# The first Strassen product of each MLP, computed ahead of the plain second matmul

## The chip, the core and the metric

The kernel runs on one core of a Trainium2 chip. The metric is device time in microseconds (us), the median of the timed runs; before the change it is 1533.13 us. Engines are named as in the profile: PE is TensorE, DVE VectorE, ACT ScalarE, POOL GpSimd, SP the queue that issues nearly all DMAs. Each engine works off its own instructions strictly in order and waits on semaphores.

## The reference

Two trunk layers run over 512 latent and 128 context tokens (640 in all, width 1024, float32). Layer 0 mixes tokens by convolution and retention, layer 1 by attention; each then has a squared-ReLU MLP, and only that is touched here:

```python
m = jax.nn.silu(cond) @ ada_w[layer] + ada_b[layer]      # six vectors of 1024: shifts, scales, gates
sh1, sc1, g1, sh2, sc2, g2 = ...
h = rmsnorm(x, norm_g[layer, 1]) * (1 + sc2) + sh2
x = x + g2 * (jnp.square(jax.nn.relu(h @ mlp_w1[layer])) @ mlp_w2[layer])   # 1024 -> 4096 -> 1024
```

The product `silu(cond) @ ada_w` of layer 1, and the gates of layer 0, are computed in small pieces between the other matmuls of layer 0. Layer 1 has none left to compute.

## The kernel before

**Three products for one.** A float32 number is kept as a high part (`wH`, `hH`, `fH`; type fp32r) and the rest (`wL`, `hL`, `fL`). A product is high·high + high·low + low·high, three matmuls. ACT copies the high part, DVE or POOL subtracts it from the raw number to get the low part. A group of 12 such matmuls of 320 columns (4 row blocks x 3) fills one PSUM bank.

**The MLP in cycles.** The 4096 hidden columns are taken in eight cycles of 512 (`CYCLES`). Cycle 0 is plain: `w1(0)`, eight groups that make 512 hidden columns, then `w2(0)`, sixteen groups that multiply them back. Cycles 1 to 6 compute both products by Strassen's scheme, with seven block products each: those on the first matrix are keyed `("p", s, i)`, those on the second `("q", s, i)`, where `i` is B11, T2, T3, T1, B22, B21, T4 in PE's order for p. T1 to T4 are sums of weight blocks that DVE makes (`add_blocks`, L2588). A p product is 24 matmuls. The last cycle is p products and a plain second matmul. The very first p product of a layer is B11 times A11 (upper left block of h); it depends on h alone, and not on the hidden columns.

**From `w1(0)` to `w2(0)`.** ACT takes the ReLU of a group (`relu`, L1770), DVE squares it (`fs`, L2522), ACT copies the high part (`hidden_hi`, L1764), DVE subtracts (`hidden_lo`, L2513, writes `fL`). The loop `hidden` on DVE does this for eight pieces n = 0 to 7; at n = 5 it also makes the low parts of tile t0+2 (the first of the two tiles of `w2(0)`; `weight_lo`, L2221), at n = 6 the first sum of h blocks (`s_raw`, L2533). PE takes piece n = 7 in the third group of `w2(0)`. After that DVE adds each of the sixteen groups to x (`update`, L2087) and between them makes the sums and low parts that the p products need (the table `after`).

**Before the fifth p product.** B22 shares banks 0 and 1 with T1, so PE may start it only when DVE has read T1's result (`combine`, L2604, writes `fq`). On DVE's list that comes behind `t_lo` of T1, B22 and B21, the sum for T4, and the first sum for the next group (`q_add(s2, T3)`, writes `t_first`), which waits for a weight block loaded into the buffer that p's B22 has freed.

**Buffers.** Raw weights land in four buffers (`raw` holds 0 and 1, `raw_high` 2 and 3), dealt in turn; high and low parts have four slots each, dealt in turn by `BLOCK_AT`. `load_raw` makes SP wait until the low part of the buffer's previous block is there.

**The ada pieces.** `ada` is one buffer of 1 MB. `load_ada(p)` (L567) waits until piece p-1 has been used; `strips(p)` on PE (L875, 16 matmuls) waits for its landing. In layer 0 pieces 16 and 17 are used behind groups 5 and 7 of `w1(0)` (`hooks`), piece 18 in the middle of `w2(0)`, and then some in every cycle. In SP's code `ada_block(1)`, which is piece 17, stands behind all four loads of `w2(0)`.

Of the kernel before, what the change touches and what calls it, by code (L numbers as in the profile page):

```python
# [46 lines left out]
PLAIN = 1  # L47
# [26 lines left out]
T_MLP0 = T_WC + 2  # L74
# [12 lines left out]
Q_ORDER = (B11, T2, T3, T4, T1, B22, B21)  # L87
SUM_ORDER = (T3, T2, T1, T4)
P_DVE = ((T1, B22, B21, T4), (T2, T3, T1, B22, B21, T4))
BLOCKS, RAW_SEQ = [], []  # L90


# [5 lines left out]
for t_ in range(N_TILES):  # L98
    layer_ = 0 if T_MLP0 <= t_ < T_QKV else 1
    c_, b_ = divmod(t_ - (T_MLP0, T_MLP1)[layer_], 4)  # L100
    if not (T_MLP0 <= t_ < T_QKV or T_MLP1 <= t_) or b_ < 2 and c_ < PLAIN or b_ > 1 and c_ not in W2:
        BLOCKS += both(t_)
        RAW_SEQ += both(t_)
    elif b_ == 0:
        BLOCKS += [("p", WINO * layer_ + c_ - PLAIN, i_) for i_ in range(7)]
        RAW_SEQ += [("p", WINO * layer_ + c_ - PLAIN, i_) for i_ in (B11, T1, B22, B21)]
    elif b_ == 2:
        BLOCKS += [("q", len(W2) * layer_ + c_ - PLAIN, i_) for i_ in Q_ORDER]
        RAW_SEQ += [("q", len(W2) * layer_ + c_ - PLAIN, i_) for i_ in (B11, T1, B22, B21)]
# [2 lines left out]
RAW_BUF, RAW_COUNT, RAW_PREV, raw_last_, raw_n_ = {}, {}, {}, [None] * 4, 0  # L112
for key_ in RAW_SEQ:
    if key_[0] in ("p", "q") or T_MLP0 <= key_[0] < T_QKV or T_MLP1 <= key_[0]:
        buf_ = raw_n_ % 4
        raw_n_ += 1
    else:
        buf_, raw_n_ = 2 * (key_[0] % 2 and key_[0] in TWO_RAW) + key_[1], 0
    RAW_BUF[key_], RAW_PREV[key_] = buf_, raw_last_[buf_]
    RAW_COUNT[key_] = 1 + (RAW_COUNT[raw_last_[buf_]] if raw_last_[buf_] else 0)  # L120
    raw_last_[buf_] = key_
# [140 lines left out]
def hybrid_step(nc, x_prompt, x_sample, state_ret, cache_k, cache_v, ada_w, even_w_in, even_w_out, final_g,  # L262
# [3 lines left out]
    with ctx:  # L266
# [274 lines left out]
        def _(sp):  # L541
# [83 lines left out]
            def load_mlp(layer, first_tile):  # L625

                def w1(c):
                    for b in range(2):
                        load_tile(first_tile + 4 * c + b, k8(mlp_w1[layer], 512 * c + 256 * b))
                        if layer == 0 and c == 0 and b == 0:  # L630
                            load_ada(M_MLP)

                def w2(c, tile, js):
                    if c < CYCLES - 1:
                        halves = [mlp_w2[layer, 512 * c:512 * (c + 1), 256 * q:256 * (q + 1)]
                                  .rearrange("(k p) n -> p k n", p=P) for q in (2 * tile, 2 * tile + 1)]
                    else:
                        halves = [mlp_w2[layer, 512 * c + 256 * (1 - j):512 * c + 256 * (2 - j), 512 * tile:512 * (tile + 1)]
                                  .rearrange("(k p) n -> p k n", p=P) for j in range(2)]
                    load_tile(first_tile + 4 * c + 2 + tile, halves, js)  # L640

                def p_block(c, row, col):

                    return (mlp_w1[layer, 512 * row:512 * (row + 1), 512 * c + 256 * col:512 * c + 256 * (col + 1)]
                            .rearrange("(k p) n -> p k n", p=P))

                def q_block(c, row, col):

                    return (mlp_w2[layer, 512 * c + 256 * row:512 * c + 256 * (row + 1), 512 * col:512 * (col + 1)]
                            .rearrange("(k p) n -> p k n", p=P))  # L650

                def ada_block(n):

                    if layer == 0:
                        load_ada(M_MLP + n)

                def first_blocks(c):

                    s = WINO * layer + c - PLAIN
                    load_raw(("p", s, B11), p_block(c, 0, 0))  # L660
                    load_raw(("p", s, T1), p_block(c, 0, 1))
                    load_raw(("p", s, B22), p_block(c, 1, 1))
                    ada_block(3 * c)
                    load_raw(("p", s, B21), p_block(c, 1, 0))

                def second_blocks(c):

                    s = len(W2) * layer + c - PLAIN
                    load_raw(("q", s, B11), q_block(c, 1, 0))
                    load_raw(("q", s, T1), q_block(c, 1, 1))  # L670
                    ada_block(3 * c + 1)
                    load_raw(("q", s, B22), q_block(c, 0, 1))
                    load_raw(("q", s, B21), q_block(c, 0, 0))
                    ada_block(3 * c + 2)

                w1(0)
                for c in range(CYCLES):
                    if c in W2:
                        second_blocks(c)
                    else:  # L680
                        if 0 < c < PLAIN:
                            ada_block(3 * c)
                        w2(c, 0, (0,))
                        if c == CYCLES - 1:
                            ada_block(3 * c + 1)
                        w2(c, 0, (1,))
                        w2(c, 1, (0,))
                        if 0 < c < PLAIN:
                            ada_block(3 * c + 1)
                        w2(c, 1, (1,))  # L690
                        if c == 0:
                            ada_block(1)
                        ada_block(3 * c + 2)
                    if c + 1 < PLAIN:
                        w1(c + 1)
                    elif c < CYCLES - 1:
                        first_blocks(c + 1)
# [49 lines left out]
        def _(pe):  # L747
# [436 lines left out]
            def first_strassen(layer, c, v, part):  # L1184
# [3 lines left out]
                def one(i, operand, bank, m, opens=True):  # L1188
                    block_product(("p", s, i), 256, 4, bank, m, operand, opens)

                wait_low(pe, "p", s, B11)
                for m in range(2):
                    if c - 1 in W2:
                        pe.wait_ge(dve_free, v - 28 + 22 + m)
                    one(B11, A11, 6 + m, m)
                part(0)
                wait_low(pe, "p", s, T2)
                pe.wait_ge(s_ready, 4 * layer + 1)
# [75 lines left out]
            def mlp(layer, norm):  # L1274
# [6 lines left out]
                for c in range(CYCLES):  # L1281
                    t, v, s = t0 + 4 * c, v0 + V_CYCLE[c], WINO * layer + c - PLAIN
                    hooks = {}
                    if c == 0:
                        if layer == 0:
                            hooks = {5: [lambda: strips(M_MLP)], 7: [lambda: strips(M_MLP + 1)]}
                        tile_pair(t, hH, hL, lambda n: pe.wait_ge(dve_free, v0 - 3 + n) if n < 4 else pe.wait_ge(act_free, a0 + n - 3),
                                  lambda half, tile, k: pe.wait_ge(h_ready, 16 * norm + 8 * half + k + 1), hooks,
                                  inside=(2, 0, lambda: stat(norm, 1, SUMS)), joint=((0, 1), (2, 3), (4, 5), (6, 7)))
                    elif c < PLAIN:  # L1290
                        for b in range(2):
                            if layer == 0:
                                hooks = {1: [lambda c=c, b=b: strips(M_MLP + 3 * c + b)]}
                            tile_t(t + b, hH, hL, lambda n: pe.wait_ge(dve_free, v - 3 + n) if b == 0 else
                                   pe.wait_ge(act_free, a0 + 8 * c + n + 1), None, hooks)
                    else:
                        first_strassen(layer, c, v, part(c))
# [166 lines left out]
        def _(act):  # L1464
# [291 lines left out]
            def mlp_layer(layer):  # L1756
# [15 lines left out]
                        hidden_hi(c, n - 1)  # L1772

                def partial(c, m, out, groups, done):
                    act.wait_ge(acc_full, g0 + G_CYCLE[c] + groups + m)
                    nc.scalar.activation(out[:, m, :], ps[:, 6 + m, 0:HALF], ACT.Copy).then_inc(done, 1)

                def partials(c, out, groups, done):
# [75 lines left out]
                    hidden_hi(0, n)  # L1854
                relu(0, 4)
                relu(0, 5)
                split(t0 + 2, g0 + 6)
                relu(0, 6)
                relu(0, 7)
                split(t0 + 3, g0 + 8)  # L1860
                hidden_hi(0, 7)
                for c in range(CYCLES):
                    t, g, s = t0 + 4 * c, g0 + G_CYCLE[c], WINO * layer + c - PLAIN
                    if 0 < c < PLAIN:
# [3 lines left out]
                            split(t + 2 + b, g + 4 * b + 4)  # L1868
                        hidden_hi(c, 7)
                    elif c:  # L1870
                        partials(c, p1, 1, p1_done)
                        if layer:
                            split_product("p", s, T1, g)
                        split_product("p", s, B22, g + 2)
# [27 lines left out]
                    if c == CYCLES - 1:  # L1902
# [7 lines left out]
                        hidden_last(F12, (0, 1))  # L1910
                        split(t + 3, g + 14, (1,))
                        break
                    for q in range(4):
                        if q == 1:
                            s_split(4, 8)
                        if c + 1 < PLAIN:
                            split(t + 4 + q // 2, g + 8 + 4 * (q + 1), (q % 2,))
                        elif q < 3 or layer == 0:
                            split_product("p", s + 1, (B11, T2, T3, T1)[q], g + 8 + 4 * (q + 1))
                        if q == 0:  # L1920
                            act.wait_ge(acc_full, g + 8)
                            s_split(1, 4)
                            s_split(3, 5)
                            s_split(2, 6)
                v0 += V_CYCLE[CYCLES - 1]
                if layer == 0:
                    before_halves_end(2, v0, T_QKV, G_QKV)
# [150 lines left out]
        def _(dve):  # L2078
# [421 lines left out]
            def mlp_layer(layer, norm):  # L2500
# [249 lines left out]

                def update(c, n):
                    half, k = (n // 8, n % 8) if c == CYCLES - 1 else (n // 2 % 2, 2 * (n // 4) + n % 2)
                    residual(g0 + G_CYCLE[c] + (8 if c < PLAIN else 14), v0 + V_CYCLE[c], n, half, k, gate_at)

                for c in range(CYCLES):
                    if c == 0:
                        hidden(0, {5: [lambda: weight_lo(t0 + 2)], 6: s_steps[0:1]})
                    elif c in W2:
                        strassen_cycle(c)
                        continue  # L2760
# [226 lines left out]
```

## Time and profile before

| | |
|---|---|
| timed runs | 1532.93, 1533.13, 1533.91 us; median 1533.13 |
| profiled execution | 1531.19 us, of which the profile's span is 1529.3 us |
| busy | PE 1499.2 us (98%), DVE 1208.6 (79%), ACT 708.8 (46%), POOL 604.0 (39%) |
| granted PE clock, mean | 0.998 of full |

Matmuls are pipelined: a matmul of 320 columns is shown with some 310 ns, but the next one starts some 147 ns later. The time between starts is therefore what counts for PE; the idle time in brackets is shorter than what a wait costs. Layer 0's MLP takes the span from about 424 to 855 us, layer 1's from about 1108 to 1520 us.

### The profile page before, as it was taken

How to read it: one execution, taken by the hardware profiler on the slowest of the kernel's cores; microseconds unless marked ns; L12 is line 12 of the kernel's file. 1: busy time of each engine (PE TensorE's matmuls, PEld its weight loads, DVE VectorE, ACT ScalarE, POOL GpSimd, SP SyncE). 2: the span in 40 equal slices, each digit the busy share in tenths (PEclk: the TensorE clock that was granted, in tenths of full speed). 3: DMA queues.
4: the chain of work that ended last, by engine and by line, in shares of the span. 5: the costliest groups of instructions: out<-in, count | busy, mean ns of one | idle time of the engine just before them, and what ended most of it. 6: DMA issues, size and time to landing. Idle time of an engine off the chain costs nothing. (4 is left out here: it accounts for less than half of the span.)

```text
span 1529.3 us, 28267 instructions
## 1 busy us (share of the span) xinstructions
PE 1499.2 (98%) x11658; PEld 1462.3 (96%) x11658; DVE 1208.6 (79%) x1925; ACT 708.8 (46%) x1162; POOL 604.0 (39%) x390
## 2 busy tenths in 40 slices
PE   8999999999999999999999999999999999999998
PEld 7999999999999999999999999999999999999998
DVE  5348678666799987897897888773599999999995
ACT  5323333334444554455455534653454445545563
POOL 0233313314323755665564253101322475447531
PEclk9999999999999999999999999999999999999999
DMA  9455334213233435433445121001222222322222
GB/s 327 162 175 170 98 95 168 74 44 117 90 126 111 139 125 180 135 127 125 139 138 164 36 84 63 29 1 56 73 66 70 83 70 77 103 83 70 84 83 83
DMA packets 121119, 162.18 MB, mean 106 GB/s; under 512 B 4640, under 2 KB 83488, under 8 KB 120992
## 3 DMA queue, kind: packets, MB, share of 16 engines
q1 hardware_dynamic: 119760, 159.34, 32.2%
q8 instruction: 92, 1.51, 0.4%
q10 hardware_dynamic: 1232, 1.05, 0.2%
q14 instruction: 35, 0.29, 0.1%
HBM read 156.44 MB, written 3.93 MB: 105 GB/s over the span
## 5 line engine op out<-in xcount | busy, mean ns | idle before, releaser
L2051 POOL TENSOR_TENSOR wL<-raw,wH 128x512 fp32r<-128x512 f32 x184 | 294.4, 1626 | 700.9 <-ACT wH L1475 484.4
L1180 PE MATMUL ps<-fx,wH 128*128 128x320 f32 x1344 | 297.5, 310 | 3.0 <-DVE held L2644 2.8
L1180 PEld LDWEIGHTS ps<-fx,wH 128*128 128x128 f32 x1344 | 224.1, 188 | 6.2 <-issue 5.9
L1180 PE MATMUL ps<-fx,wL 128*128 128x320 f32 x672 | 207.6, 309 | 0.0
L756 PE MATMUL ps<-hH,wH 128*128 128x320 f32 x576 | 181.4, 315 | 1.9 <-DVE hL L2137 1.3
L756 PE MATMUL ps<-hH,wL 128*128 128x320 f32 x576 | 178.0, 309 | 0.0
L756 PE MATMUL ps<-hL,wH 128*128 128x320 f32 x576 | 177.9, 309 | 0.0
L2051 POOL TENSOR_TENSOR wL<-raw_high,wH 128x512 fp32r<-128x512 f32 x92 | 130.5, 1445 | 95.7 <-ACT wH L1475 78.8
L756 PE MATMUL ps<-wH,hH 128*128 128x256 f32 x560 | 162.1, 289 | 2.4 <-DVE hL L2137 2.1
L756 PE MATMUL ps<-wL,hH 128*128 128x256 f32 x560 | 158.3, 283 | 0.0
L756 PE MATMUL ps<-wH,hL 128*128 128x256 f32 x560 | 158.3, 283 | 0.0
L1180 PE MATMUL ps<-s,wH 128*128 128x320 f32 x672 | 150.4, 312 | 3.2 <-DVE fq L2604 2.9
L1180 PE MATMUL ps<-hL,wH 128*128 128x320 f32 x448 | 138.5, 309 | 0.0
L1180 PE MATMUL ps<-hH,wL 128*128 128x320 f32 x448 | 138.5, 309 | 0.0
L1180 PE MATMUL ps<-hH,wH 128*128 128x320 f32 x448 | 138.4, 309 | 0.0
L1180 PEld LDWEIGHTS ps<-fx,wL 128*128 128x128 f32 x672 | 126.2, 188 | 0.0
L2051 POOL TENSOR_TENSOR wL<-t_second,wH 128x512 fp32r<-128x512 f32 x60 | 101.7, 1716 | 52.9 <-ACT wH L1493 52.7
L1180 PEld LDWEIGHTS ps<-s,wH 128*128 128x128 f32 x672 | 111.5, 188 | 7.8 <-issue 6.0
L756 PEld LDWEIGHTS ps<-hH,wH 128*128 128x128 f32 x576 | 108.2, 188 | 6.0 <-DVE hL L2137 2.8
L756 PEld LDWEIGHTS ps<-wH,hH 128*128 128x128 f32 x560 | 107.2, 191 | 3.6 <-DVE xT L2087 1.4
L2087 DVE SCALAR_TENSOR_TENSOR xT<-ps,modT,xT 128x320 f32<-128x320 f32 (+2 forms) x168 | 66.8, 432 | 55.4 <-PE ps L756 55.1
L756 PEld LDWEIGHTS ps<-hL,wH 128*128 128x128 f32 x576 | 108.2, 188 | 0.2
(305 smaller groups left out, 3853.5 us busy)
## 6 DMA issues: line engine op xcount, KB each, us to landing
ada<-in_ada_w SPq DMA_DIRECT2D x40, 1024.0 KB, 5.9
raw<-in_mlp_w SPq DMA_DIRECT2D x64, 512.0 KB, 3.7
raw_high<-in_mlp_w SPq DMA_DIRECT2D x64, 512.0 KB, 3.8
raw<-in_even_w_in SPq DMA_DIRECT2D x28, 512.0 KB, 5.8
pre_w<-in_ada_w SPq DMA_DIRECT2D x16, 512.0 KB, 9.2
raw<-in_odd_w_qkv SPq DMA_DIRECT2D x10, 512.0 KB, 3.7
raw<-in_even_w_out SPq DMA_DIRECT2D x8, 512.0 KB, 3.6
raw<-in_odd_w_o SPq DMA_DIRECT2D x6, 512.0 KB, 3.5
```

What stands on the lines that cost most here:

```text
L756: last = nc.tensor.matmul(ps[:, bank, 0:width], a_, b_, start=(k == 0 and p_ == 0), stop=(k == nk - 1 and p_ == 2))
L1180: last = nc.tensor.matmul(ps[:, bank, 0:HALF], a_, b_, start=(opens and k == 0 and p_ == 0), stop=(k == nk - 1 and p_ == 2), skip_group_ch ...
L2051: last = nc.gpsimd.tensor_tensor(wL[:, at % 4, cs], source(key)[:, cs], wH[:, at % 4, cs].bitcast(F32), ALU.subtract)
L2087: last = nc.vector.scalar_tensor_tensor(out=x, in0=ps[:, n % 4, c0 - half * HALF:c0 - half * HALF + w_], scalar=modT[:, gate_at + k, which ...
```

## The change

- PE: the product B11·A11 of the first p group moves from behind `w2(0)` to its front, in both layers.
- SP: its raw block is loaded right behind the blocks of `w1(0)`, ahead of those of `w2(0)`. For the first twelve blocks of a layer's MLP the table `SEAM_BUF` deals the raw buffers, then a fixed turn. The second half of tile t0+3 thereby comes into buffer 1, behind the first half of t0+2. It was in buffer 3, behind a block of `w1(0)`.
- Slots: B11 takes the slot that the first half of t0+2 had, and each of the four halves of `w2(0)` moves on by one.
- ACT: B11's high part comes first of the weights; of t0+2 only the first half is made there, the second behind the last `hidden_hi`, which moves ahead of tile t0+3. The copy of the B11 result (`partials(PLAIN, p1, ...)`) comes behind the high parts of T2 and T3.
- DVE: the low part of t0+2's second half moves from n = 5 of `hidden` to behind `hidden`.

```diff
+SECOND_TILES = (T_MLP0 + 1, T_MLP1 + 1)
+SEAM_BUF = (0, 1, 2, 3, 0, 1, 2, 3, 1, 2, 3, 1)
...
+        if t_ in SECOND_TILES:
+            BLOCKS.append(("p", WINO * layer_, B11))
+            RAW_SEQ.append(("p", WINO * layer_, B11))
...
-        buf_ = raw_n_ % 4
+        buf_ = SEAM_BUF[raw_n_] if raw_n_ < len(SEAM_BUF) else (0, 2, 3, 1)[raw_n_ % 4]
...
                 w1(0)
+                load_raw(("p", WINO * layer, B11), p_block(PLAIN, 0, 0))
...
+                        wait_low(pe, "p", WINO * layer, B11)
+                        for m in range(2):
+                            block_product(("p", WINO * layer, B11), 256, 4, 6 + m, m, A11, True)
...
-                split(t0 + 2, g0 + 6)
+                split_product("p", WINO * layer, B11, g0 + 6)
+                split(t0 + 2, g0 + 6, (0,))
                 relu(0, 6)
                 relu(0, 7)
-                split(t0 + 3, g0 + 8)
                 hidden_hi(0, 7)
+                split(t0 + 2, g0 + 8, (1,))
+                split(t0 + 3, g0 + 8, (0,))
+                split(t0 + 3, g0 + 10, (1,))
...
-                        hidden(0, {5: [lambda: weight_lo(t0 + 2)], 6: s_steps[0:1]})
+                        hidden(0, {5: [lambda: weight_lo(t0 + 2, (0,))], 6: s_steps[0:1]})
+                        weight_lo(t0 + 2, (1,))
```

SP's list at the start of layer 0's MLP, before. The first row is the first half of the blocks of `w1(0)`; `ada` is a piece of the ada weights, `raw` and `raw_high` are the raw buffers, and the semaphore in brackets is what SP waits for ahead of a transfer.

```order
L550 DMA raw<-in_mlp_w 128x4x256 [waits wl_done] x2
L567 DMA ada<-in_ada_w 128x4x512 [waits ada_strips]
L550 DMA raw_high<-in_mlp_w 128x4x256 [waits wl_done] x2
L550 DMA raw<-in_mlp_w 128x4x256 [waits wl_done] x2
L550 DMA raw_high<-in_mlp_w 128x4x256 [waits wl_done] x2
L567 DMA ada<-in_ada_w 128x4x512 [waits ada_strips] x2
L550 DMA raw<-in_mlp_w 128x4x256 [waits dve_wl] x2
L550 DMA raw_high<-in_mlp_w 128x4x256 [waits wl_done]
```

The same piece of SP's list now:

```order
L556 DMA raw<-in_mlp_w 128x4x256 [waits wl_done] x2
L573 DMA ada<-in_ada_w 128x4x512 [waits ada_strips]
L556 DMA raw_high<-in_mlp_w 128x4x256 [waits wl_done] x2
L556 DMA raw<-in_mlp_w 128x4x256 [waits wl_done] x2
L556 DMA raw_high<-in_mlp_w 128x4x256 [waits wl_done] x2
L556 DMA raw<-in_mlp_w 128x4x256 [waits dve_wl]
L573 DMA ada<-in_ada_w 128x4x512 [waits ada_strips] x2
L556 DMA raw_high<-in_mlp_w 128x4x256 [waits dve_wl]
```

The two loads of ada pieces 17 and 18 stood behind transfers that wait for POOL's low parts only. Now a transfer that waits for `dve_wl`, DVE's low part of t0+2's first half, stands ahead of them.

ACT's list in both layers from the last `relu` pair but one to the sums of h, before (`fr` is `relu`, `fH` is `hidden_hi`, L1475 the high part of a plain block, L1493 that of a p block):

```order
L1475 ACTIVATE wH<-raw 128x1024 [waits raw_in0,acc_full]
L1475 ACTIVATE wH<-raw 128x1024 [waits raw_in1]
L1770 ACTIVATE fr<-ps 128x320 [waits fs_done,acc_full]
L1764 ACTIVATE fH<-fs 128x320 [waits fs_done]
L1770 ACTIVATE fr<-ps 128x320 [waits fs_done,acc_full]
L1764 ACTIVATE fH<-fs 128x320 [waits fs_done]
L1475 ACTIVATE wH<-raw_high 128x1024 [waits raw_in2,acc_full]
L1475 ACTIVATE wH<-raw_high 128x1024 [waits raw_in3]
L1764 ACTIVATE fH<-fs 128x320 [waits fs_done]
L1493 ACTIVATE wH<-raw 128x1024 [waits raw_in0,acc_full]
```

And now:

```order
L1504 ACTIVATE wH<-raw 128x1024 [waits raw_in0,acc_full]
L1486 ACTIVATE wH<-raw 128x1024 [waits raw_in1,acc_full]
L1781 ACTIVATE fr<-ps 128x320 [waits fs_done,acc_full]
L1775 ACTIVATE fH<-fs 128x320 [waits fs_done]
L1781 ACTIVATE fr<-ps 128x320 [waits fs_done,acc_full]
L1775 ACTIVATE fH<-fs 128x320 [waits fs_done] x2
L1486 ACTIVATE wH<-raw_high 128x1024 [waits raw_in2,acc_full]
L1486 ACTIVATE wH<-raw_high 128x1024 [waits raw_in3,acc_full]
L1486 ACTIVATE wH<-raw 128x1024 [waits raw_in1,acc_full]
```

B11's high part has moved from the last row to the first, the last `fH` from behind the weights of t0+3 to ahead of them, and the rest of the weights of `w2(0)` behind it.

## Rows read from the trace of the kernel before

**Rows 1.** The page: busy time of each engine, share of the span.

```profile
PE 1499.2 (98%) x11658; PEld 1462.3 (96%) x11658; DVE 1208.6 (79%) x1925; ACT 708.8 (46%) x1162; POOL 604.0 (39%) x390
```

**Rows 2.** Timeline of PE, layer 0: start, us, instruction, idle before.

```profile
446.53 1.08 PE L875 MATMUL ps<-ada,siluc 128*32 128x128 f32 x32
...
452.42 0.30 PE L756 MATMUL ps<-fH,wL 128*128 128x320 f32 x1
453.50 0.41 PE L756 MATMUL ps<-fH,wH 128*128 128x320 f32 x1 [0.78 <-DVE fL L2513]
...
482.76 0.56 PE L1180 MATMUL ps<-s,wH 128*128 128x320 f32 x2
...
494.53 0.56 PE L1180 MATMUL ps<-s,wH 128*128 128x320 f32 x2
```

**Rows 3.** Timeline of PE, layer 1.

```profile
1129.93 0.31 PE L756 MATMUL ps<-fH,wH 128*128 128x320 f32 x1
...
1135.50 0.41 PE L756 MATMUL ps<-fH,wH 128*128 128x320 f32 x1 [1.01 <-DVE fL L2513]
...
1136.98 0.41 PE L756 MATMUL ps<-fH,wH 128*128 128x320 f32 x1 [0.78 <-DVE fL L2513]
...
1163.93 0.46 PE L1180 MATMUL ps<-s,wH 128*128 128x320 f32 x2
...
1175.15 0.54 PE L1180 MATMUL ps<-s,wH 128*128 128x320 f32 x2 [0.50 <-DVE fq L2604]
```

**Rows 4.** Timeline of SP, layer 0: start of the first, to the end of the last.

```profile
439.42 8.62 SPq L567 DMA_DIRECT2D ada<-in_ada_w  x2
```

**Rows 5.** Tile ada, 439 to 447 us: landing of its one transfer.

```profile
DMA to landing us min/median/max: 5.0/5.0/5.0
```

**Rows 6.** Tile ada, 483 to 490 us: a transfer issued close behind another one.

```profile
DMA to landing us min/median/max: 5.9/5.9/5.9
```

**Rows 7.** Timeline of ACT: high parts of t0+2 in layer 0 and layer 1.

```profile
441.54 1.99 ACT L1475 ACTIVATE wH<-raw 128x1024 fp32r<-128x1024 f32 x2
...
1126.24 1.99 ACT L1475 ACTIVATE wH<-raw 128x1024 fp32r<-128x1024 f32 x2
```

**Rows 8.** Timeline of DVE, layer 0: a low part beside POOL's work and one alone.

```profile
478.37 1.25 DVE L2087 SCALAR_TENSOR_TENSOR xT<-ps,modT,xT 128x192 f32<-128x192 f32 x4
...
480.94 2.31 DVE L2553 TENSOR_TENSOR wL<-raw,wH 128x1024 fp32r<-128x1024 f32 x1
...
486.09 1.22 DVE L2553 TENSOR_TENSOR wL<-raw_high,wH 128x1024 fp32r<-128x1024 f32 x1
...
493.57 0.49 DVE L2604 TENSOR_TENSOR fq<-ps,u 128x320 f32<-128x320 f32 x1
```

**Rows 9.** Timeline of POOL: low parts alone, and beside DVE's.

```profile
412.69 5.07 POOL L2051 TENSOR_TENSOR wL<-raw,wH 128x512 fp32r<-128x512 f32 x4 [20.63 <-ACT wH L1475]
...
479.57 4.82 POOL L2051 TENSOR_TENSOR wL<-t_begin,wH 128x512 fp32r<-128x512 f32 x2
```

**Rows 10.** Timeline of PE behind its longest wait.

```profile
22.46 0.49 PE L961 MATMUL ps<-hH,wH 128*128 128x320 f32 x1 [3.58 <-DVE hL L2137]
...
25.69 0.46 PE L961 MATMUL ps<-hH,wH 128*128 128x320 f32 x1
25.96 0.33 PE L961 MATMUL ps<-hL,wH 128*128 128x320 f32 x1
```

**Rows 11.** Windows: stretch, its length, PE busy, granted clock, DMA share, GB/s.

```profile
22.40:26.00 3.60, 3.54 (x14) 0.53 1.10 348
```

**Rows 12.** Timeline of DVE, layer 1, up to the fifth p product.

```profile
1161.71 0.67 DVE L2087 SCALAR_TENSOR_TENSOR xT<-ps,modT,xT 128x192 f32<-128x192 f32 x2
...
1165.54 1.23 DVE L2553 TENSOR_TENSOR wL<-raw,wH 128x1024 fp32r<-128x1024 f32 x1 [0.64 <-ACT wH L1493]
...
1173.38 1.23 DVE L2588 TENSOR_TENSOR t_first<-raw_high,raw 128x1024 f32<-128x1024 f32 x1 [1.67 <-DMA raw_high<-in_mlp_w]
1174.52 0.48 DVE L2604 TENSOR_TENSOR fq<-ps,u 128x320 f32<-128x320 f32 x1
```

More of the change, by code:

```diff
@@ L103 @@
         RAW_SEQ += both(t_)
+        if t_ in SECOND_TILES:
+            BLOCKS.append(("p", WINO * layer_, B11))
+            RAW_SEQ.append(("p", WINO * layer_, B11))
     elif b_ == 0:
-        BLOCKS += [("p", WINO * layer_ + c_ - PLAIN, i_) for i_ in range(7)]
-        RAW_SEQ += [("p", WINO * layer_ + c_ - PLAIN, i_) for i_ in (B11, T1, B22, B21)]
+        loaded_ = 1 if c_ == PLAIN else 0
+        BLOCKS += [("p", WINO * layer_ + c_ - PLAIN, i_) for i_ in range(loaded_, 7)]
+        RAW_SEQ += [("p", WINO * layer_ + c_ - PLAIN, i_) for i_ in (B11, T1, B22, B21)[loaded_:]]
     elif b_ == 2:
@@ L659, in first_blocks @@
                     s = WINO * layer + c - PLAIN
-                    load_raw(("p", s, B11), p_block(c, 0, 0))
+                    if c > PLAIN:
+                        load_raw(("p", s, B11), p_block(c, 0, 0))
                     load_raw(("p", s, T1), p_block(c, 0, 1))
@@ L1189, in one @@
                     block_product(("p", s, i), 256, 4, bank, m, operand, opens)
-                wait_low(pe, "p", s, B11)
-                for m in range(2):
-                    if c - 1 in W2:
+                if c > PLAIN:
+                    wait_low(pe, "p", s, B11)
+                    for m in range(2):
                         pe.wait_ge(dve_free, v - 28 + 22 + m)
-                    one(B11, A11, 6 + m, m)
+                        one(B11, A11, 6 + m, m)
                 part(0)
@@ L1289, in mlp @@
                                   inside=(2, 0, lambda: stat(norm, 1, SUMS)), joint=((0, 1), (2, 3), (4, 5), (6, 7)))
+                        wait_low(pe, "p", WINO * layer, B11)
+                        for m in range(2):
+                            block_product(("p", WINO * layer, B11), 256, 4, 6 + m, m, A11, True)
                     elif c < PLAIN:
@@ L1774, in partial @@
                 def partial(c, m, out, groups, done):
-                    act.wait_ge(acc_full, g0 + G_CYCLE[c] + groups + m)
+                    act.wait_ge(acc_full, g0 + (8 if out is p1 and c == PLAIN else G_CYCLE[c]) + groups + m)
                     nc.scalar.activation(out[:, m, :], ps[:, 6 + m, 0:HALF], ACT.Copy).then_inc(done, 1)
@@ L1870, in mlp_layer @@
                     elif c:
-                        partials(c, p1, 1, p1_done)
+                        if c > PLAIN:
+                            partials(c, p1, 1, p1_done)
                         if layer:
@@ L1912, in mlp_layer @@
                         break
[L1913 to L1924, printed above, removed]
+                    s_split(1, 4)
+                    s_split(3, 5)
+                    s_split(2, 6)
+                    s_split(4, 8)
+                    split_product("p", s + 1, T2, g + 14)
+                    split_product("p", s + 1, T3, g + 18)
+                    partials(PLAIN, p1, 1, p1_done)
+                    if layer == 0:
+                        split_product("p", s + 1, T1, g + 22)
                 v0 += V_CYCLE[CYCLES - 1]
@@ L2752, in update @@
                     half, k = (n // 8, n % 8) if c == CYCLES - 1 else (n // 2 % 2, 2 * (n // 4) + n % 2)
-                    residual(g0 + G_CYCLE[c] + (8 if c < PLAIN else 14), v0 + V_CYCLE[c], n, half, k, gate_at)
+                    residual(g0 + G_CYCLE[c] + (10 if c < PLAIN else 14), v0 + V_CYCLE[c], n, half, k, gate_at)
                 for c in range(CYCLES):
                     if c == 0:
-                        hidden(0, {5: [lambda: weight_lo(t0 + 2)], 6: s_steps[0:1]})
+                        hidden(0, {5: [lambda: weight_lo(t0 + 2, (0,))], 6: s_steps[0:1]})
+                        weight_lo(t0 + 2, (1,))
                     elif c in W2:
```

## The prediction

> **What bounds the kernel now.** I read the page first, then the timeline of PE around the two places where the change sits, then SP, ACT, POOL and DVE in the same stretches, and last the one place where PE stood still for long. PE is busy 98% of the span [rows 1]. No work is taken from it, so all that can be won is its waiting, and all that can be lost is new waiting. In layer 0 PE starts a matmul at 452.42 and the next at 453.50, because DVE's last `fL` is late [rows 2]. That is 1.08 us where 0.15 is normal, and the first matmul behind a wait takes 0.1 more: 1.0 us lost. The row shows 0.78 idle, so a wait costs its idle time plus some 0.25. In layer 1 the same thing happens twice, with 1.01 and 0.78 idle [rows 3], together 2.3 us. These 3.3 us are the whole prize, 0.22% of 1533. DVE is the second engine to watch: around the change it works without a break, and in layer 1 PE's fifth product, B22, already waits for it (0.50 idle before 1175.15, released by `fq`) [rows 3].
>
> **The change part by part.** The order of PE's list is as announced: 24 matmuls of B11 in front of `w2(0)`, 24 x 0.147 = 3.5 us of the same work at another place. By itself that costs nothing, and it gives DVE 3.5 us more before its last `fL` is wanted. I take the 1.0 and the 2.3 us as won: the last `fL` was 1 to 2 us late, and one of the two low parts of t0+2 (1.2 us) has also left its way.
>
> *SP's queue in layer 0* is where I see the price. Ada piece 17 is loaded at 439.42 [rows 4], lands 5.0 us later [rows 5], at 444.4, and PE uses it at 446.53 without a wait [rows 2]. Reserve: 2.1 us. Now the load of t0+3's second half stands ahead of it on SP, and this one waits for DVE's low part of t0+2's first half, because it has been dealt that block's buffer. When is that low part there? ACT makes two high parts from 441.54 on, 1.99 us together [rows 7]. B11's is now the first, so that of t0+2 is done at 443.5. DVE then needs 1.2 us alone or 2.3 beside POOL [rows 8], and POOL is on B11 just then. That gives 444.8 to 445.8. SP issues the weight block (0.4 us) and then the ada piece, at 445.2 to 446.2. Its landing takes 5.0 us alone [rows 5] and 5.9 close behind another transfer [rows 6], as here. So it lands between 450.2 and 452.1, and PE, which is due at 446.53, waits 3.7 to 5.6 us. Behind these 16 matmuls on PE's list stand B11, `w2(0)` and all the rest, and nothing else can run on PE. I take 5.4, near the upper end, since both contentions apply.
>
> *The clock behind that wait.* After 3.58 us of idle time PE came back at 22.46, and thirteen starts took until 25.96 [rows 10], 0.27 us apart in place of 0.147. The granted clock of that stretch is 0.53 [rows 11], so nearly all of it was at the lower level, 1.2 of 2.4 GHz. The loss was 3.50 - 13 x 0.147 = 1.6 us. A wait of 5.4 us is longer, so I add 1.6 (ends: 0, if the clock holds, and 1.6). The Trainium skill, "TensorE: Matmul & The Clock Gate", section "What's actually happening", says that the throttled state is the default and that activity releases it. By that rule the term stays; if the clock did not follow idle time, the sum would be 1.6 less.
>
> *B11's low part.* In layer 0 ACT hands B11 over at 442.6. POOL needs two pieces, 1.27 us each alone and 2.4 beside DVE [rows 9]: there by 445.1 to 447.4, hidden behind the ada wait. In layer 1 no ada matmuls stand between, and PE is due at 1129.93 [rows 3]. ACT's first copy ends at 1127.3 [rows 7], so POOL is done at 1129.8 to 1132.1, a new wait of 0 to 2.2 us. The first piece runs mostly alone, the second beside DVE's low part: 1.3 + 2.4, 1131.0. I take 1.1.
>
> *DVE behind `w2(0)`.* Until now B11 stood between `w2(0)` and T2, and DVE used its 3.5 us to catch up. Now its last addition to x comes only after the last group of `w2(0)` (0.3 us to notice, 0.7 to do), and T2 follows at once. In layer 0 DVE took from the end of that addition, 479.62, to the end of `fq`, 494.06 [rows 8], 14.4 us. The stretch holds low parts, sums, and a transfer that can only start when B22's low part is done. So `fq` is ready 15.4 us after `w2(0)`. PE would be ready for B22 after an ada piece of 1.1 and the 11.8 us from 482.76 to 494.53 [rows 2], 12.9 in all. That is 2.5 late. Some of DVE's stretches beside POOL get shorter, since POOL starts T2 and T3 earlier, so I take 2.0 (ends: 0 and 2.6). In layer 1 it took from 1162.38 to 1175.01 [rows 12], 12.6, of which 0.64 was a wait for ACT's T1 that goes, since T1's high part is made earlier against the rest. With 1.0 in front and 0.1 behind: 13.1 us, against 11.2 on PE from 1163.93 to 1175.15 [rows 3], its old wait included: 1.9 more (ends: 0.65 less, when PE needs only its three products of 3.5 us, and 2.6 more).
>
> *At nothing.* The second half of t0+2 comes later on ACT and DVE, but PE wants it only in the fifth group of `w2(0)`, 10 us after the start of B11. The copies of the B11 result move behind T2 and T3 on ACT, whose gaps there cover them; were they late, T2 would wait 0.4 us. In the groups that follow, the raw buffers have new numbers and the same waits, so I expect no difference.
>
> The sum: layer 0, 5.4 + 1.6 - 1.0 + 2.0 = 8.0; layer 1, 1.1 - 2.3 + 1.9 = 0.7; together 8.7 us. On the profiled execution that is 1531.2 + 8.7 = 1539.9. The median of the timed runs is 1.9 above that execution: 1533.1 + 8.7 = 1541.8 us.
>
> **The rivals.** *PE is the only bound.* Then all that stands beside it has room: SP is not held, DVE keeps step, and the waits for `fL` go: -1.0 - 2.3 - 0.65 = -3.95, 1529.2 us. The 98% of PE speaks for it. It is decided at one point, whether the ada piece lands by 446.53. That needs its issue by 441.5, before ACT has even begun the high part on which it now depends. I give it 0.05.
>
> *The wait alone.* The ada piece is late by 5.4, but the clock holds and DVE has its work done when PE needs it: 5.4 - 1.0 + 1.1 - 2.3 = 3.2, 1536.3 us. For it: DVE has 2 us of waiting for transfers in these stretches, which may shrink. Against it: that transfer hangs on B22's low part, which is itself late. 0.15.
>
> *Everything at its lower end.* Ada wait 3.7, clock holds, POOL alone, DVE on time: 3.7 - 1.0 - 2.3 - 0.65 = -0.25, 1532.9 us. 0.06.
>
> *The clock falls three times.* PE's new waits of about 2 us before B22 in both layers bring the lower level too, 1.6 each: 8.7 + 3.2 = 11.9, 1545.0 us. Between 1.0 us of idle, after which the rows show normal starts, and 3.58 the trace shows nothing. 0.12.
>
> **How the numbers follow.** The forecast, 1541.8, has the remaining 0.62. Within it the ada wait moves the time by 2 down and 0.2 up, DVE's two terms by 4.5 down and 1.3 up, POOL's by 1.1 either way. The range 1536.0 to 1545.5 takes in those, the wait alone and the third fall of the clock, and leaves out 0.11 and a little at its ends. What this kernel's runs can tell from no change is about 0.2%, 3.1 us. Faster by more: 0.05. Within: the lower end and a part of the wait alone, 0.06 + 0.05 = 0.11. Slower: 0.84.
>
> **What would show it.** In the profile of the changed kernel the 16 ada matmuls at some 447 us carry an idle time of 4 to 6 us, released by the ada transfer, and this transfer's issue stands at 445 to 446 and not at 439. The granted clock falls once behind it. The three waits for `fL` are gone. B11 in layer 1 waits about 1 us for POOL, and the fifth product about 2 us for `fq` in both layers. If the ada matmuls do not wait, the forecast is wrong by 7 us, and if the fifth products do not, by 4.

## The result, and the profile after

The changed kernel takes 1543.62 us (median of 4 runs, 1540.74 to 1545.43) against 1533.52 for the kernel before. The ratio is 1.0074, 95% interval 1.0063 to 1.0086: slower by 10.1 us, where 8.7 were forecast. The profiled execution took 1542.1 us with a span of 1540.2, so 10.9 more of span than before. The page's busy line, answering to [rows 1], shows that PE has about as much to do and more time to do it in:

```profile
PE 1503.4 (98%) x11658; PEld 1466.9 (95%) x11658; DVE 1197.8 (78%) x1925; ACT 708.5 (46%) x1162; POOL 600.8 (39%) x390
```

PE's busy time grew by 4.2 us with the same 11658 matmuls: some of them ran slower. The rest is waiting. PE's list of waits over the whole span (first what waits and for whom, then the total, the number and the longest):

```profile
PE ps L1188 <- DVE fq L2616: 7.2, 7, 2.8
PE ps L883 <- DMA ada<-in_ada_w: 4.9, 2, 4.7
...
PE ps L1188 <- POOL wL L2063: 0.8, 1, 0.8
```

The row for `fL`, 2.6 us in three waits before, is not there any more. In layer 0 the timeline of PE answers to [rows 2] (start, us, instruction, idle before it and its releaser):

```profile
451.93 1.93 PE L883 MATMUL ps<-ada,siluc 128*32 128x128 f32 x32 [4.67 <-DMA ada<-in_ada_w]
453.80 0.64 PE L1188 MATMUL ps<-hH,wH 128*128 128x320 f32 x1
...
456.10 0.47 PE L1188 MATMUL ps<-hH,wL 128*128 128x320 f32 x1
456.37 0.35 PE L1188 MATMUL ps<-hH,wH 128*128 128x320 f32 x1
...
500.08 1.08 PE L883 MATMUL ps<-ada,siluc 128*32 128x128 f32 x32 [0.19 <-DMA ada<-in_ada_w]
503.95 0.65 PE L1188 MATMUL ps<-s,wH 128*128 128x320 f32 x2 [2.79 <-DVE fq L2616]
```

SP's timeline answers to [rows 4]. The weight block goes out at 445.74, when DVE's low part of t0+2 is there, and the ada piece only behind it:

```profile
445.74 0.37 SPq L556 DMA_DIRECT2D raw<-in_mlp_w  x1
446.15 8.15 SPq L573 DMA_DIRECT2D ada<-in_ada_w  x2
```

The windows behind the two long waits, a normal stretch, and the stretch behind layer 1's wait (length, busy times of PE, PEld, DVE, ACT, POOL, then the granted clock):

```profile
451.90:456.60 4.70, 4.67 (x43) 4.18 (x44) 2.00 (x3) 0.53 (x1) 2.60 (x2) 0.52 0.31 78
456.60:461.20 4.60, 4.60 (x33) 4.60 (x32) 0.64 (x2) 1.06 (x1) 1.27 (x2) 1.00 1.06 371
503.90:507.70 3.80, 3.75 (x15) 3.78 (x16) 3.64 (x4) 1.59 (x3) 0.63 (x1) 0.55 0.00 0
1184.90:1188.60 3.70, 3.17 (x20) 2.94 (x21) 3.70 (x3) 1.17 (x2) 3.21 (x2) 1.00 0.00 0
```

In the MLPs the clock stands near half twice, at the lower of its two levels, 1.2 and 2.4 GHz: behind 4.67 and behind 2.79 us of idle time. Behind 1.50 us, in layer 1, it stays at 1.00. PE's waits there answer to [rows 3]:

```profile
1140.47 0.42 PE L1188 MATMUL ps<-hH,wH 128*128 128x320 f32 x1 [0.84 <-POOL wL L2063]
...
1172.61 0.56 PE L1188 MATMUL ps<-s,wH 128*128 128x320 f32 x2 [0.19 <-DVE wL L2565]
1184.93 0.53 PE L1188 MATMUL ps<-s,wH 128*128 128x320 f32 x2 [1.50 <-DVE fq L2616]
1187.42 0.56 PE L1188 MATMUL ps<-s,wH 128*128 128x320 f32 x2 [0.49 <-DVE fq L2616]
```

And DVE ahead of `fq` in layer 0, answering to [rows 8]. Between B22's chain and `fq` it stands still for 2.85 us, until a transfer lands:

```profile
497.31 1.22 DVE L2600 TENSOR_TENSOR raw<-raw,t_first 128x1024 f32<-128x1024 f32 x1
501.38 2.02 DVE L2600 TENSOR_TENSOR t_first<-raw_high 128x1024 f32<-128x1024 f32 x1 [2.85 <-DMA raw_high<-in_mlp_w]
503.33 0.48 DVE L2616 TENSOR_TENSOR fq<-ps,u 128x320 f32<-128x320 f32 x1
```

Matching the n-th matmul of the one trace with the n-th of the other gives the ledger of the 10.9 us (the difference of their starts, before and behind each place):

| place | forecast | measured |
|---|---|---|
| start of the kernel, up to 28 us | 0 | +0.7 |
| layer 0: ada wait | +5.4 | +4.7 |
| layer 0: half clock behind it | +1.6 | +1.9 |
| layer 0: `fL` wait | -1.0 | -1.0 |
| layer 0: B22, with ada piece 20 ahead of it | +2.0 | +4.6, of it 1.4 half clock |
| around 762 us, a later group of layer 0 | 0 | -1.3 |
| layer 1: `fL` waits gone, B11 waits for POOL | -2.3 + 1.1 | -1.2 |
| layer 1: T2 and B22 | +1.9 | +1.9 |
| layer 1: later groups | 0 | +0.7 |

The -1.3 are two waits of the kernel before, 0.42 and 0.56 us idle at 760.39 and 762.95, which this execution doesn't have. They also go in kernels below that leave that place alone, so they aren't put down to the change. The same holds for the start: from 16.2 to 19.5 us this execution had a granted clock of 0.50, and the one before had 1.00. The rounded rows add up to 11.0.

### The profile page after: what moved, and what is told of

Its sections match the earlier page's. It is cut to its first block and busy times, and to the rows that moved or that the text cites. A ratio compares the mean times of both kernels' runs of the same rounds, so it can differ in the third digit from the quotient of the medians.

```text
span 1540.2 us, 28269 instructions
## 1 busy us (share of the span) xinstructions
PE 1503.4 (98%) x11658; PEld 1466.9 (95%) x11658; DVE 1197.8 (78%) x1925; ACT 708.5 (46%) x1162; POOL 600.8 (39%) x390
## 5 line engine op out<-in xcount | busy, mean ns | idle before, releaser
L2063 POOL TENSOR_TENSOR wL<-raw,wH 128x512 fp32r<-128x512 f32 x188 | 285.9, 1549 | 746.5 <-ACT wH L1486 486.7
L2063 POOL TENSOR_TENSOR wL<-raw_high,wH 128x512 fp32r<-128x512 f32 x88 | 139.1, 1606 | 49.8 <-ACT wH L1486 41.4
L1188 PEld LDWEIGHTS ps<-s,wH 128*128 128x128 f32 x672 | 112.6, 190 | 12.3 <-issue 10.1
```

The costliest lines, as they stand in the source:

```text
L1188: last = nc.tensor.matmul(ps[:, bank, 0:HALF], a_, b_, start=(opens and k == 0 and p_ == 0), stop=(k == nk - 1 and p_ == 2), skip_group_ch ...
L2063: last = nc.gpsimd.tensor_tensor(wL[:, at % 4, cs], source(key)[:, cs], wH[:, at % 4, cs].bitcast(F32), ALU.subtract)
```

## The experiments

**The ada piece alone.** On SP's queue its load goes back in front of the waiting weight block:

```diff
+                        if c == 0:
+                            ada_block(1)
                         w2(c, 1, (1,))
-                        if c == 0:
-                            ada_block(1)
```

> The changed kernel with one line moved: on SP's queue the load of ada piece 17 stands ahead of the load of t0+3's second half again. Theory (the queue): the piece is issued at about 440, as soon as piece 16 is used, lands by 445, and PE does not wait for it at 447. The wait of 4.7 us and the half clock behind it (about 1.7 us) go: 1543.6 - 6.4 = 1537.2 us. Rival (the wait is only passed on): B11's low part, the weights of t0+2 or DVE's fL are late next, since DVE and POOL are full there; then PE waits at one of these and the time falls by 3 us at most, to 1540.6 or more. Third: the clock fell for another reason than the wait; then only 4.7 us go, 1538.9.

Measured: 1536.08 us, ratio to the kernel before (1532.83) 1.0024, interval 1.0012 to 1.0035. The piece goes out at 440.57 and PE does not wait. Set against the changed kernel, 7.5 us are back, 1.1 more than expected:

```profile
440.57 0.37 SPq L573 DMA_DIRECT2D ada<-in_ada_w  x1
446.22 0.37 SPq L556 DMA_DIRECT2D raw<-in_mlp_w  x1
```

No other wait takes its place at 447. So the queue was the cause of two thirds of the loss (0.0050 of 0.0074 by the ratios). But the kernel is still 3.3 us slower than before, though its `fL` waits are gone too.

**The same delay in the kernel before.** SP waits for DVE's low part ahead of the ada piece, nothing else:

```diff
                         if c == 0:
+                            if layer == 0:
+                                wait_low(sp, first_tile + 2, 1)
                             ada_block(1)
```

> The kernel before, with SP held ahead of the load of ada piece 17 until DVE has made the low part of t0+2's second half (at 445.0 there); nothing else is moved. Theory: the piece is issued at 445.1 and lands at 450.1, PE waits 3.5 us at 446.5, its clock falls and costs 1.6 more, and the wait for the last fL (1.0) goes, since DVE gets the time: 1533.5 + 3.5 + 1.6 - 1.0 = 1537.6. Rival (the clock holds over a wait of this length): 1536.0. Rival (the ada piece is not what PE waits for): 1533.5, no change.

Measured: 1535.76 us, ratio 1.0031 (1.0020 to 1.0041), so 2.9 us more than the kernel before in the same comparison (1532.83), between the rival's 2.5 and the theory's 4.1. The seven times lie in two groups, 1535.0 to 1535.8 and 1538.8 to 1539.1, and the profile is one of the upper, 1538.8:

```profile
451.08 1.94 PE L877 MATMUL ps<-ada,siluc 128*32 128x128 f32 x32 [3.51 <-DMA ada<-in_ada_w]
452.94 0.64 PE L758 MATMUL ps<-fH,wH 128*128 128x320 f32 x1
453.38 0.47 PE L758 MATMUL ps<-fL,wH 128*128 128x320 f32 x1
```

The wait is 3.51 as worked out, the starts behind it are 0.27 us apart, and at this place the execution loses 5.1 us net, with the `fL` wait of layer 0 gone. That shows that the wait and the half clock at this place come from the late piece alone. Of the 7.6 us between the two profiles the rest is not the edit's work. The start of the kernel took 1.0. In layer 1, which the edit leaves as it was, PE waits for `fL` as in [rows 3], 1.02 and 0.78 us, but this time half clock follows and costs 1.5 us (PE, then the window behind it):

```profile
1143.00 0.64 PE L758 MATMUL ps<-fH,wH 128*128 128x320 f32 x1 [0.78 <-DVE fL L2515]
...
1143.00:1146.40 3.40, 3.40 (x13) 3.40 (x14) 3.40 (x6) 0.00 (x0) 1.08 (x1) 0.50 0.65 200
```

So the same two waits came at full clock in one execution and with half clock in another. The mean granted clocks of the seven runs point the same way for the two groups, 0.994 to 0.995 in the upper and 0.995 to 0.997 in the lower; no profile of the lower group shows where.

**The two `fq` ahead of the transfer.** In the first Strassen group DVE makes both `fq` before the sums that need the late transfer:

```diff
-                    q_add(s2, T3)
+                    if c > PLAIN:
+                        q_add(s2, T3)
                     combine(c, F11, 0)
-                    q_add(s2, T2)
+                    if c > PLAIN:
+                        q_add(s2, T2)
                     combine(c, F11, 1)
+                    if c == PLAIN:
+                        q_add(s2, T3)
+                        q_add(s2, T2)
```

> The changed kernel with DVE's list in the first Strassen group of each MLP reordered: the two sums fq that free the banks of B22 stand ahead of the two sums for the second matmul's T3 and T2, the first of which waits for a transfer. Theory: the fifth product waits for DVE only because DVE itself stands waiting for that transfer with the ready fq behind it. Then the wait before B22 goes, in layer 0 2.8 us and the half clock behind it, 1.6, in layer 1 1.7 and 0.55: 1543.6 - 6.6 = 1537.0 us. Rival (DVE has simply too much to do there): the sums for T3 and T2 come later, the low part of T4 and the operands of the second matmul with them, and PE waits there instead: 1541 to 1544.

Measured: 1543.2 us, ratio 1.0069 (1.0055 to 1.0082): nothing gained. The theory falls. The waits for `fq` at B22 are gone from both layers, and in their place stands, in layer 1, the second product of the second matmul, which waits for DVE's copy `held` of the first (timeline of PE, then of DVE ahead of it, then the window behind it):

```profile
1199.40 0.87 PE L1188 MATMUL ps<-fx,wH 128*128 128x320 f32 x2 [2.99 <-DVE held L2654]
```

```profile
1195.02 0.88 DVE L2633 TENSOR_TENSOR u<-fq 128x640 f32<-128x640 f32 x1 [0.95 <-ACT fq L1816]
1195.82 2.30 DVE L2600 TENSOR_TENSOR t_second<-raw,t_second 128x1024 f32<-128x1024 f32 x1
1198.04 0.81 DVE L2642 TENSOR_TENSOR fx<-u,fx 128x640 fp32r<-128x640 f32 x1
1198.78 0.87 DVE L2654 COPY held<-ps 128x320 f32<-128x320 f32 x2
```

```profile
1199.30:1205.30 6.00, 5.90 (x22) 5.93 (x23) 3.96 (x8) 1.87 (x3) 5.58 (x4) 0.50 0.01 3
```

The first copy is done at 1199.25, the last of a row of DVE's work, while PE has started its last matmul at 1196.1. The two short waits (1.50 and 0.49) became one of 2.99, and behind it the clock was at 0.50 for 6 us, which the short ones had not cost in the changed kernel's profile. In layer 0 the fifth product does start without a wait and at full clock, as the theory says, but PE now waits 1.83 us for ada piece 20 ahead of it and 0.6 for `held` behind it. By matched starts layer 0 gains 1.9 us on the changed kernel and layer 1 loses 3.3.

**Both edits.** The diffs of the first and the third run together.

> The changed kernel with both edits: ada piece 17 loaded ahead of t0+3's second half, and the two fq ahead of the sums for T3 and T2. Theory: the two costs stand apart, so both go: 1543.6 - 6.4 - 6.6 = 1530.6 us, 2.9 under the kernel before, which is the prize of the three fL waits (3.3) and of the old wait for fq (0.6), less the wait for POOL's B11 in layer 1 (1.0). Rival (B11 in front overloads DVE and POOL at the seam whatever the order): 1533.5 or more.

Measured: 1536.35 us, ratio 1.0024 (1.0014 to 1.0035), as with the ada piece alone. The number fits the rival: with the `fq` first, PE waits 3.0 us for `held` in layer 1 and 1.9 for ada piece 20 in layer 0. This 1.91 brings half clock, where the 1.83 at the same place, in the run with the `fq` edit alone, did not (PE, then the window behind it):

```profile
495.58 1.41 PE L883 MATMUL ps<-ada,siluc 128*32 128x128 f32 x32 [1.91 <-DMA ada<-in_ada_w]
...
496.20:499.60 3.40, 3.40 (x30) 3.01 (x19) 2.62 (x2) 0.73 (x1) 1.15 (x1) 0.50 0.01 4
```

**B22's low part sooner.** With the ada piece mended, DVE makes B22's low part ahead of that of S4, so that the transfer behind it can start:

```diff
                     if c == PLAIN:
+                        t_lo(s, B22)
                         s_low(4, 4)
                     modulate(c, 0)
-                    t_lo(s, B22)
+                    if c > PLAIN:
+                        t_lo(s, B22)
                     t_lo(s, B21)
```

> The changed kernel with ada piece 17 ahead of t0+3's second half (as in the run of 1536.1 us), and in the first Strassen group DVE makes B22's low part ahead of the low part of S4 (1.5 us). Theory (the transfer behind B22's low part is what PE waits for): that transfer starts 1.5 us sooner in both layers, fq is ready 1.5 us sooner, and the waits before the fifth product shrink by as much: 1536.1 - 3.0 = 1533.1 us, a little less where the clock then holds. Rival (the reordering of DVE only passes the wait on, as with the two fq ahead, to the second matmul's T2, whose operand is DVE's): 1536.

Measured: 1536.54 us, ratio 1.0031 (1.0020 to 1.0041): no gain. In layer 1 the wait for `fq` is 1.1 in place of 1.9 us. In layer 0 it is 2.8 against 2.6, since the transfer, issued sooner, now runs close behind ada's 1 MB and takes 7.8 us in place of 6.6. So a second reordering of DVE passes the wait on or meets a transfer.

**Idle work in the place that B11 left.** If PE just gets to the fifth product too soon, then 3.5 us of useless matmuls per layer must be free:

```diff
                 pe.wait_ge(s_ready, 4 * layer + 1)
+                if c == PLAIN:
+                    ...   # the 24 matmuls of T2, into bank 5
                 for m in range(2):
```

> The changed kernel with ada piece 17 ahead of t0+3's second half (1536.1 us), and 24 idle matmuls more per layer: the product T2 is computed once into a bank that nobody reads, between the second matmul and T2, the place that B11 has left (3.5 us of PE each time, 7.0 in all). Theory (since B11 has left, PE reaches the fifth product before DVE and its transfer do): the idle matmuls lie in time in which PE stands still anyway. In layer 0 E1's profile shows 4.4 us of waiting there and the half clock, in layer 1 2.2 us and some half clock, so the 7.0 us cost -1 to +1: 1535 to 1537 us. Rival (PE is the bound at the seam, and the waits there are accidents): 1536.1 + 7.0 = 1543.

Measured: 1534.96 us, ratio 1.0022 (1.0013 to 1.0031). 48 matmuls more, 7.0 us of PE, and the time is not above the 1536.08 without them. The two were timed in different comparisons, so the ratios to the kernel before are what counts: 1.0022 with and 1.0024 without, each known to about 0.001, or 1.5 us, far less than 7.0. PE's waits from 440 to 530 us without the idle work:

```profile
PE ps L1188 <- DVE fq L2616: 2.6, 1, 2.6
PE ps L883 <- DMA ada<-in_ada_w: 1.6, 1, 1.6
```

With it this list is empty, and in layer 1 the 1.9 us for `fq` are gone as well; only these stay (1128 to 1205 us):

```profile
PE ps L1188 <- POOL wL L2071: 0.8, 1, 0.8
PE ps L1213 <- DVE wL L2573: 0.2, 1, 0.2
```

This shows what B11 did at its old place: between `w2(0)` and T2 it covered DVE's and the transfers' time for the next products. In front of `w2(0)` it covers nothing there.

**The prize without moving B11.** The kernel before, with DVE's first S sum behind the last `fL`, and ACT's last `fH` ahead of t0+3's high parts:

```diff
-                        hidden(0, {5: [lambda: weight_lo(t0 + 2)], 6: s_steps[0:1]})
+                        hidden(0, {5: [lambda: weight_lo(t0 + 2)]})
+                        s_steps[0]()
...
-                split(t0 + 3, g0 + 8)
                 hidden_hi(0, 7)
+                split(t0 + 3, g0 + 8)
```

> The kernel before with B11 left where it was. DVE's first sum of S (1.48 us) stands behind the last fL and not two places ahead of it, and ACT's last fH stands ahead of the high parts of t0+3. Theory (the three fL waits come from DVE's and ACT's own order): the last fL is 1.5 us sooner in layer 0 and 1.5 to 2 sooner in layer 1, and most of the 3.3 us goes without moving any matmul: 1532.8 - 2.9 = 1529.9 us. Rival (DVE has no room at the seam): the sum is late for S1 to S4 or for the first additions to x, and PE waits for these: 1532.8 or more.

Measured: 1527.14 us, ratio 0.9968 (0.9957 to 0.9979), 5.2 us under the kernel before (1532.37), where 2.9 were forecast; the interval goes from 3.2 to 6.6 us. No wait for `fL` is left.

**The same with B22's low part sooner.** The diff of B22's low part on top of the last one.

> The kernel before with the sum of S behind the last fL, the last fH ahead of t0+3's high parts, and B22's low part ahead of the low part of S4 in the first Strassen group. Theory: besides the fL waits the 0.5 us wait for fq before the fifth product of layer 1 goes: 1529.4 us. Rival: S4's low part is late in its turn and the fifth product waits for it: 1530 to 1531.

Measured: 1527.82 us, ratio 0.9972 (0.9963 to 0.9982). The wait for `fq` in layer 1 (0.8) goes and one of 0.6 for `held` in the second matmul comes: nothing gained.

**Which of the two edits.** DVE's move alone (the first hunk above):

> The kernel before with DVE's part of the last edit alone: the first sum of S stands behind the last fL; ACT is as before. Theory (DVE's order is the cause): fL is up to 1.5 us sooner, the waits of 1.0 in layer 0 and 1.25 in layer 1 go, of the second one in layer 1 up to 0.6 stays, since the last fH stands behind t0+3's high parts: 1532.4 - 2.5 = 1529.9 us. Rival (it is ACT's order that counts): 1532.

Measured: 1531.22 us, ratio 0.9990 (0.9981 to 0.9999), just clear of no change. What is won at `fL` is mostly lost behind it. DVE's last `fL` in layer 0 waits for ACT's `fH`, which stands behind t0+3's high parts, and is slow; the sum comes behind it, and PE waits for DVE's first addition to x:

```profile
450.89 1.63 DVE L2513 TENSOR_TENSOR fL<-fs,fH 128x320 fp32r<-128x320 f32 x1 [1.41 <-ACT fH L1764]
...
456.71 0.42 PE L756 MATMUL ps<-fH,wH 128*128 128x320 f32 x1 [0.94 <-DVE xT L2087]
```

ACT's move alone (the second hunk):

> The kernel before with ACT's part alone: the last fH stands ahead of the high parts of t0+3; DVE is as before. Theory (DVE's order is the cause): the last fH waits for fs, which DVE makes behind the sum of S, so nothing is gained: 1532.4 us. Rival (POOL beside DVE is the cause): t0+3's high parts come later, so POOL's low parts start later and DVE's last two short steps run alone, 0.5 in place of 1.6 us each; then most of the fL waits go all the same: 1529 to 1530.

Measured: 1527.20 us, ratio 0.9966 (0.9952 to 0.9980): as much as both moves together, and by the rival's mechanism. The kernel before, DVE and then POOL in layer 0:

```profile
447.48 1.48 DVE L2533 TENSOR_TENSOR s_raw<-hH,hL 128x1280 f32<-128x1280 f32 x1
448.88 1.59 DVE L2522 TENSOR_TENSOR fs<-fr 128x320 f32<-128x320 f32 x1
450.39 3.06 DVE L2513 TENSOR_TENSOR fL<-fs,fH 128x320 fp32r<-128x320 f32 x2
...
448.70 5.90 POOL L2051 TENSOR_TENSOR wL<-raw_high,wH 128x512 fp32r<-128x512 f32 x4 [25.95 <-ACT wH L1475]
```

And with ACT's move alone (this execution is 1.7 us later at this point):

```profile
449.14 1.49 DVE L2533 TENSOR_TENSOR s_raw<-hH,hL 128x1280 f32<-128x1280 f32 x1
450.54 0.49 DVE L2522 TENSOR_TENSOR fs<-fr 128x320 f32<-128x320 f32 x1
450.94 1.11 DVE L2513 TENSOR_TENSOR fL<-fs,fH 128x320 fp32r<-128x320 f32 x2
...
452.56 6.31 POOL L2051 TENSOR_TENSOR wL<-raw_high,wH 128x512 fp32r<-128x512 f32 x3 [28.14 <-ACT wH L1475]
```

With the `fH` in front, ACT waits for DVE before it hands t0+3 to POOL. So POOL starts when DVE has finished its last short steps, and these take 0.49 us in place of 1.5 to 1.6. In layer 1 it is the same, 0.48 in place of 1.59 for the last `fs`. The Trainium skill, "SBUF — State Buffer", section "SBUF: two separate sides", says that DVE and GpSimd share one port pair as an exclusive lock, and the other one waits for a whole instruction. The trace agrees: 1.59 is 1.10 more than 0.49, a little under one POOL piece alone (1.27 [rows 9]). The DVE move alone leaves POOL's start at 449.63, and its last `fL` still takes 1.63.

By matched starts of the two profiles the `fL` waits are worth 1.1 us in layer 0 and 2.3 in layer 1, which is the prize that the prediction names. The medians differ by 5.8 us, with an interval from 3.1 to 7.4. What the rest is, is not shown; the half clock that the `fL` waits brought in the run with the ada piece late may be a part of it.

The changed kernel has ACT's move among its own: "last high part sooner". So the one part of it that a run shows to gain by itself was bundled with two that cost more: the ada piece behind the waiting load, and the place that B11 left.

## Why the prediction was right, and where it was not

The profile lost 10.9 us of span where 8.7 were forecast. The three places for which nothing was forecast (+0.7, -1.3, +0.7) cancel, which is luck. The 2.2 us that are left lie in the terms: 0.7 less for the ada wait, 0.3 more for its half clock, 2.6 more for B22 in layer 0.

- **The ada wait and SP's queue**: right. 4.7 against 5.4; issue at 446.15 (forecast 445.2 to 446.2), landing after 5.7 us (forecast 5.0 to 5.9). Shown from both sides: taken away in the changed kernel, it gave back 7.5 us; put into the kernel before, PE waited 3.51.
- **The clock behind it**: right, 1.9 against 1.6. The granted clock was 0.52 behind the wait and 1.00 behind further work. The Trainium skill, "TensorE: Matmul & The Clock Gate", section "What's actually happening", with its rule that activity releases the throttle, agrees with that order.
- **B22 in layer 0**: right in mechanism, mis-sized. The step set DVE 2.5 us late and took 2.0, because "Some of DVE's stretches beside POOL get shorter". It was 2.79 idle, since DVE stood still for 2.85 us for the transfer where it had waited 1.9 before, and the clock fell behind it too (1.4 us). That is half of the rival "the clock falls three times", which was given 0.12. In layer 1, where the wait was 1.50, the clock held. Rows of before could not have settled it, and by the other runs a wait near 1.9 us goes either way (behind 1.91 it fell, behind 1.83 and 1.87 it held).
- **Layer 1**: right in sum (0.7 forecast, 0.7 up to the end of that group), with POOL's wait of 0.84 idle and DVE's 1.50 and 0.49 as forecast.
- **Where the prize comes from**: right in size, the cause not separated. The prediction took the three `fL` waits as won by B11's 3.5 us of cover, and gave the move of ACT's last `fH` no term. Either would have been enough. With ACT's move alone the waits are gone (1527.20 against 1533.02). With PE merely later, in the run with the ada piece late, the wait of layer 0 is gone without ACT's move; for layer 1 the traces allow only an estimate: in the kernel before the last `fL` is there 7.1 us behind the last start of `w1(0)`, PE asks for it at 5.0 where it does not wait, and with 3.5 of cover at 8.5. What the prediction missed is that the prize was to be had without moving B11. The trace of before had it: `fs` of 1.59 beside POOL, where 0.49 is normal.
- **"By itself that costs nothing"**, of B11's new place: the matmuls cost nothing, but the place they left does. The prediction had it as DVE's term; the idle matmuls show how large it is: in the kernel with the ada piece mended, 7 us of PE work there are free.
- **Later groups with no difference**: right within what the executions vary by, +0.7 and -1.3.

What remains open: where the lower group of times with the delayed ada piece saves its clock, and how the 3.3 us that stay after mending the ada piece divide between the layers. The one profile of that kernel loses 4.7 us in layer 0 and 0.7 in layer 1, each up to B22, with the gain at `fL` counted in; but it is of the slowest of six runs, and the waits in layer 0 differ between executions with the landing of ada piece 20 (6.1 to 8.2 us).

## What to carry to other kernels

Matmuls that seem to stand at any place are cover for the engines that prepare the next ones; before moving them, ask who needs their time where they stand now. A load that gets a new buffer brings its buffer's wait to everything behind it on its queue. And when a short step is late, look first whether it is slow: what made it slow here could be started 2 us later by exchanging two lines on a third engine.

## What the runs showed of the hardware

- No idle length divides the waits behind which the clock fell from those behind which it held. It fell behind 2.79 us (0.55 in the stretch behind it) and 1.91 (0.50); it held behind 1.50 (1.00) and 1.83. The same two waits of 1.0 and 0.78 us came at full clock in one execution and with 0.50 behind them in another, at a cost of 1.5 us.
- Ada's transfer of 1 MB, issued 0.4 us behind a weight block, took between 5.7 and 8.2 us from one kernel to the next, and its issue 0.5 or 1.0 to 1.3 us.
- DVE's 128x320 step takes 0.49 us alone and 1.5 to 1.6 while POOL makes 128x512 pieces.
